# Two small and two large moves in the on-chip memory plan: the split-weight buffers w_hi and w_lo begin at other byte addresses

## The reference, cut to what matters

```python
def swiglu(x, w_gate, w_up, w_down):
    return (jax.nn.silu(x @ w_gate) * (x @ w_up)) @ w_down
...
    for l in range(DEPTH):
        x = x + 0.5 * swiglu(rmsnorm(x, norm_w[l, 0]), ffn_w_gate[l, 0], ffn_w_up[l, 0], ffn_w_down[l, 0])
        h = rmsnorm(x, norm_w[l, 1])
        ...
        x = x + y
        x = x + 0.5 * swiglu(rmsnorm(x, norm_w[l, 2]), ffn_w_gate[l, 1], ffn_w_up[l, 1], ffn_w_down[l, 1])
    out = rmsnorm(x, final_norm_w)
```

## Time and profile before

| | us |
|---|---|
| runs | 2196.39, 2197.02, 2197.16 |
| median | 2197.02 |
| span of the profiled execution | 2198.8 |
| TensorE busy in it | 2160.5 |
| VectorE busy | 1555.5 |
| ScalarE busy | 951.1 |

### The profile page before, as it was taken

How to read it: one execution, slowest core, us unless ns; L and a number is a source line. 1 busy time by engine, 2 the same in 40 slices (tenths; PEclk the granted TensorE clock), 3 DMA queues, 4 the chain that set the end, 5 groups by cost and what they waited for, 6 DMA issues and landing times.

```text
span 2198.8 us, 40702 instructions
## 1 busy us (share of the span) xinstructions
PE 2160.5 (98%) x16360; PEld 2137.4 (97%) x16360; DVE 1555.5 (71%) x2379; ACT 951.1 (43%) x1495; POOL 45.7 (2%) x50
## 2 busy tenths in 40 slices
PE   7999999999999999999999999999999999999997
PEld 7999999999999999999999999999999899999997
DVE  6898657685555798848679984863776457988485
ACT  5435435454433444515445452544322434445252
POOL 0000000001100000000000000000011100000000
PEclk9999999999999999999999999999999999999999
DMA  5222322224332232222323232232122222223222
GB/s 186 68 88 95 115 67 86 96 82 137 99 118 85 68 102 82 95 87 89 104 70 94 86 96 96 82 101 94 44 96 84 97 77 84 90 87 104 77 86 73
DMA packets 72578, 201.58 MB, mean 92 GB/s; under 512 B 7268, under 2 KB 26980, under 8 KB 72448
## 3 DMA queue, kind: packets, MB, share of 16 engines
q1 hardware_dynamic: 72448, 199.80, 28.1%
HBM read 187.82 MB, written 11.95 MB: 91 GB/s over the span
## 4 chain that ended last, share of the span: by engine, by line
PE 91%; DVE 5%; ACT 2%; issue 1%; DMA 0%; POOL 0%; SPq 0%; DVEq 0%; POOLq 0%
PE ps L479 48%; PE ps L536 32%; PE ps L753 4%; PE ps L608 1%; DVE w_lo L1768 1%; PE ps L784 1%; PE ps L773 1%; PE ps L787 0%; DVE w_lo L1753 0%; PE ps L803 0%; PE ps L617 0%; PE ps L796 0%; PE ps L631 0%; PE ps L797 0%; DMA x<-in_x 0%
## 5 line engine op out<-in xcount | busy, mean ns | idle before, releaser
L479 PE MATMUL ps<-h_lo,w_hi 128*128 128x288 f32 x1616 | 347.0, 294 | 4.1 <-DVE h_hi L2267 4.1
L479 PE MATMUL ps<-h_hi,w_hi 128*128 128x288 f32 x1616 | 346.5, 294 | 0.7 <-DVE w_lo L1753 0.7
L536 PE MATMUL ps<-th_hi,w_hi 128*128 128x288 f32 x1088 | 320.2, 294 | 2.4 <-ACT scratch L1219 2.4
L536 PE MATMUL ps<-th_lo,w_hi 128*128 128x288 f32 x1088 | 320.9, 295 | 0.0
L536 PE MATMUL ps<-th_hi,w_lo 128*128 128x288 f32 x1088 | 319.8, 294 | 0.0
L479 PE MATMUL ps<-h_hi,w_lo 128*128 128x288 f32 x1360 | 290.2, 292 | 0.0
L479 PE MATMUL ps<-xn_hi,w_hi 128*128 128x288 f32 x1152 | 257.2, 300 | 11.6 <-DVE w_lo L1753 8.9
L479 PEld LDWEIGHTS ps<-h_lo,w_hi 128*128 128x128 f32 x1616 | 259.9, 188 | 4.8 <-DVE h_hi L2267 4.5
L479 PEld LDWEIGHTS ps<-h_hi,w_hi 128*128 128x128 f32 x1616 | 259.9, 188 | 1.0 <-DVE w_lo L1753 0.9
L1753 DVE TENSOR_TENSOR w_lo<-raw,w_hi 128x1024 fp32r<-128x1024 f32 x196 | 232.2, 1221 | 36.9 <-ACT w_hi L1185 35.1
L479 PE MATMUL ps<-xn_hi,w_lo 128*128 128x288 f32 x1152 | 251.9, 296 | 0.0
(11 more groups left out here) (288 smaller groups left out, 4119.7 us busy)
## 6 DMA issues: line engine op xcount, KB each, us to landing
raw<-in_w_gate SPq DMA_DIRECT2D x88, 512.0 KB, 3.4
raw<-in_w_up SPq DMA_DIRECT2D x88, 512.0 KB, 4.2
raw<-in_w_down SPq DMA_DIRECT2D x64, 512.0 KB, 3.6
raw<-in_w_mix SPq DMA_DIRECT2D x64, 512.0 KB, 4.2
raw<-in_w_down SPq DMA_DIRECT2D x32, 384.0 KB, 3.2
state_s<-in_state_c SPq DMA_DIRECT2D x4, 1024.0 KB, 7.5
out_c_s<-state_s SPq DMA_DIRECT2D x4, 1024.0 KB, 4.6
state_s<-in_state_g SPq DMA_DIRECT2D x4, 1024.0 KB, 6.1
```

The costliest lines, as they stand in the source:

```text
L479: ins = nc.tensor.matmul(o, a, b[:, c] if c is not None else b, start=first and j == 0, stop=last and j == 2)
L536: ins = nc.tensor.matmul(ps[:, bank, FIRST], left, b_, start=first and k == 0 and j == 0, stop=k == KT_X // 2 - 1 and j == 2, skip_group_c ...
```

## The change

One small buffer of 128 bytes per partition, n_in, is allocated between raw and w_hi. Three small ones, head_w (64 bytes), m_in (32) and rstd_tok (20), are allocated between w_lo and h_hi. All four stood further behind before. No instruction, loop, wait or DMA is added, removed or reordered.

By the shapes the addresses become: w_hi 72960 and w_lo 89344, both 0 modulo 256 (they were at 128); h_hi, h_lo, qt, kt, og, th_hi, v_tok, scratch and rstd 256 bytes further, the same modulo 256; cst, level_mask, conv_w, conv_in, conv_out, late_stage, gate_hi and gate_lo 160 bytes further; m_out, bc, cols, w_a2 and b_a 128 further; everything from n_out on (th_lo, state, k_tok_b and others) where it was. x, xn_hi, xn_lo and raw stay.

```diff
         raw = sb("raw", [P, 4, KT_X * P])
+        n_in = sb("n_in", [P, N_HEADS, DEC_BATCH])
         w_hi, w_lo = sb("w_hi", [P, 4, KT_X * P], f32r), sb("w_lo", [P, 4, KT_X * P], f32r)
+        head_w = sb("head_w", [P, 2, KT_X])
+        m_in = sb("m_in", [N_HEADS, DEC_BATCH])
+        rstd_tok = sb("rstd_tok", [P, TT])
...
-        rstd_tok = sb("rstd_tok", [P, TT])
         norm_w = sb("norm_w", [P, N_NORMS, KT_X])
-        head_w = sb("head_w", [P, 2, KT_X])
...
-        m_in = sb("m_in", [N_HEADS, DEC_BATCH])
...
-        n_in = sb("n_in", [P, N_HEADS, DEC_BATCH])
```

## The result

The changed kernel took 2212.74 us (median of 4 runs, 2210.72 to 2215.67) beside 2197.09 us for the kernel before. The ratio is 1.007, with a 95% interval of 1.0055 to 1.0084: 15.7 us slower. The profiled execution spans 2212.9 us, 14.1 more than that of before.

What follows compares the result with a forecast made beforehand. TensorE's distance from one matmul to the next was taken to bound the kernel. Terms 0 + 0.7 + 0 + 0 + 0 = +0.7 us on the median 2197.0 gave 2197.7 us, range 2173 to 2213.

Steps and rivals of the forecast that it cites:

- the case that did not come: Whole kernel: no rhythm of the matmul stream changes, 2197.0 to 2198.3 us; chance 0.42.
- case D: Interleaved D phases fall from the 130.0 to the 133.3 ns rhythm: 4,800 x 3.3 = 15.8 us slower, 2212.9; chance 0.24.
- What bounds the kernel: TensorE, busy 2160.5 of 2198.8 us at full clock; the end moves almost only with the distance between matmuls.
- Part 1: w_hi and w_lo as stationary operands, from 128 to 0 modulo 256: taken as 0, bounds -2.1 and +3.3 ns.
- quick third gate tile: First mixer's gate products: the tile with high part at 0 modulo 256 takes 131.7 ns a matmul, against 132.9 over all 48.
- case C: Every matmul loading w at 128 stalls on one more 256-byte block; at 4 ns on 14,250 matmuls 57 us faster, 2140; chance 0.08.
- Part 2, the relation of the two streams: Seven-product form: like positions modulo 256 of moving operand and weights are quick, unlike slow; they swap, +1.3 us or 0, taken +0.7.
- Part 2, the interleaved form: Line 479's matmuls: each weight tile meets both token halves equally, so swapping like and unlike leaves the sum unchanged.
- Case D's reason: The 130.0 stretches hold because halves meet weights like, unlike; swapped to unlike, like, the stream falls into the 133.3 rhythm.
- Parts 3 to 5: Line 753's 960 matmuls (at most +1.5 us), ScalarE's and VectorE's writes into w (under 1 us), moved small buffers (0.7 us): each taken as 0.
- the argument from the slope: VectorE's splits into w: 1.04 ns a column; a port that suffered from the place would show there, and nothing does.
- The prediction's other comparison: Interleaved matmuls: a page's formula gives 122.5 ns against 130.0; if 7.5 ns were all the weights' place, about 107 us back.

Runs made afterwards that it cites:

- the first experiment: The changed kernel with all four small buffers ahead of w_hi, so w_hi and w_lo are back at 128 modulo 256: 2198.73 us, ratio 1.0009.

## Why the prediction was right, and where it was not

The forecast of 2197.7 us was the case that did not come. What came is case D, given 0.24, at its place, by its price and nearly at its time: 2212.9 was worked out, 2212.74 measured. The range held the time; its upper end of 2213.0 had nothing to spare, and two of the four runs lie above it. That it fits so well is partly luck: see the size below.

- **What bounds the kernel.** Right. The loss is TensorE's distance from start to start, at unchanged counts. The clock was misread as granted in full in every slice: a digit 9 does not say so, and the windows at 1748 us and like it are at the lower level in part. That left the forecast as it was, since both kernels have such stretches.
- **Part 1, w's own place.** Taken as 0, and shown to be 0 by the run with everything 128 bytes lower. The quick third gate tile, on which case C rested, was no sign of a quicker load; what made it quick was not looked into.
- **Part 2, the relation of the two streams.** Right in the seven-product form: the halves changed places by 1.6 to 2.1 ns, 3.16 to 3.21 us and 1.60 to 1.58. The term of +1.3 us, of which the sum took half, came to 1.8 us.
- **Part 2, the interleaved form.** Here the step failed: "each tile meets both halves equally, so the sum stays". The costs of two matmuls don't add; the alternation has a rhythm of its own, 130.0 ns, below both single costs (131.7 and 133.3), and turning the order round loses it. The prediction saw the two rhythms in the earlier trace rows and still set the sum of this form at zero in the forecast. The numbers needed for D were all there: single costs of 131.7 and 133.3 cannot make 130.0 by adding, which should have told that order matters.
- **Case D's size.** 4,800 x 3.3 = 15.8 us, against 16.1 us in the D phases and the late G stretches of the traces. Right. That the whole time then came out at 2212.7 is luck: the seven-product form added 1.8 us, which the figure of 2212.9 leaves out, shorter waits took 1.0 back, and the medians carry the clock's spread.
- **Case D's reason.** Half right. Order decides in the long stretches, as the swapped halves show. But "the stream falls" is not forced by the order alone: D phases with the old distances were slow in two runs, and the changed kernel itself has a short stretch with unlike, like at 130 ns, in the first OUT block (0.26 us a pair), where the kernel before with like, unlike takes 0.26 or 0.27:

```profile
650.25 0.42 PE L479 MATMUL ps<-h_hi,w_hi 128*128 128x288 f32 x2
650.51 0.42 PE L479 MATMUL ps<-h_lo,w_lo 128*128 128x288 f32 x2
650.77 0.42 PE L479 MATMUL ps<-h_lo,w_hi 128*128 128x288 f32 x2
```

- **Case D's counterargument,** that the eleven D phases are quick without exception, was weak: they all have the same way in, so they are one observation and not eleven.
- **Parts 3 to 5.** v_tile was bounded by +1.5 us and taken as 0; it gained some 0.5 us (below). VectorE's split of 1024 columns takes 1220 ns, against 1221; the argument from the slope could not have shown this, since it had one place only. The moved small buffers cost nothing, by the first experiment.
- **The pages.** The Trainium skill's rule on descriptors ("DMA: Bandwidth & Descriptors", "How a descriptor splits into AXI transactions") could be looked at by the way: with everything 128 bytes lower, raw too begins at a multiple of 256, and the time of the kernel did not move. The row of the gate weights, of the page of that kernel:

```profile
raw<-in_w_gate SPq DMA_DIRECT2D x88, 512.0 KB, 3.4
```

It is 3.4 us in the kernel before too. The up weights land in 3.8 us instead of 4.2, but they do so in the changed kernel as well, where raw has not moved. No gain of the rule is seen here, where no DMA is on the chain that ended last. The prediction's other comparison was set beside the wrong thing. The section "Back-to-back issue gap" of "TensorE: Matmul & The Clock Gate" in the Trainium skill gives its formula for an isolated matmul, without a budget for the weight load. The 7.5 ns by which 130.0 lies above it therefore said nothing of the weights' place, and the run with all 128 bytes lower shows that none of them came back by w's own place.

What stays open is the mechanism inside TensorE. That both operands are read from the same memory at the same time, and meet or miss each other there, fits the distances, but no row shows a read. "TensorE: Matmul & The Clock Gate", section "Step-by-step: what each phase is for", of the Trainium skill says that the moving operand and the weight load have ports of their own and that loading the next tile takes no bandwidth from the running matmul. The runs don't show a port; they show that the pace depends by up to 3.3 ns a matmul, 2.5%, on how far the two operands lie apart, which that rule does not lead one to expect. Open too is what in the way in chooses the rhythm, and why QK cannot be brought to the quick one by the means that served OUT.

## What to carry to other kernels

Where TensorE is busy 98% of the time, moving a buffer is a change to its inner loop: compare the distance from one matmul's start to the next before and after, stretch by stretch, and change the layout by 128 bytes or swap two interleaved halves as a cheap trial in both directions. What counts is where two operands lie to each other, not whether one of them begins at a round address. And where two costs alternate, don't add them: a stream of pairs can be quicker than either alone, or as slow as the slower.

## What the runs showed of the hardware that was not expected

- Two paces for the same instructions on the same addresses, 130.0 and 133.3 ns, that hold for hundreds of matmuls once taken; in OUT the slow one was turned into the quick one by 48 matmuls in another order ahead of it.
- All 128 bytes lower: 0.02% (within the interval). w alone 128 bytes further, against the rest: 0.7%. xn alone: 0.9%.
- v_tile, where w moves and xn stands (256 columns), likes other distances than the rest. First and last start of 72 matmuls in a row, of the kernel before, of the changed kernel, and with w 192 bytes further:

```profile
478.84 0.36 PE L753 MATMUL ps<-w_hi,xn_hi 128*128 128x256 f32 x1
...
487.44 0.28 PE L753 MATMUL ps<-w_lo,xn_hi 128*128 128x256 f32 x1
```

```profile
483.40 0.36 PE L753 MATMUL ps<-w_hi,xn_hi 128*128 128x256 f32 x1
...
491.91 0.28 PE L753 MATMUL ps<-w_lo,xn_hi 128*128 128x256 f32 x1
```

```profile
481.11 0.37 PE L753 MATMUL ps<-w_hi,xn_hi 128*128 128x256 f32 x1
...
489.25 0.28 PE L753 MATMUL ps<-w_lo,xn_hi 128*128 128x256 f32 x1
```

8.60, 8.51 and 8.14 us for 71 distances are 121.1, 119.9 and 114.6 ns. Over all of v_tile's stretches in the mixers the mean distance is 119.6, 119.0 and 115.2 ns: by an estimate from these, 0.5 us less in the changed kernel and 4 us less at 192 bytes, for 960 matmuls. So a place of w that costs the D phases time can be good for another form of the same kernel.
- The lower level of the clock comes and goes between executions behind one and the same wait: after 2.06 us without work it was at 0.66 of full speed on average over 5 us in one, at 1.00 in the other, 1.45 us apart.
